# Memory keys as fp32 products in two other places, and values ahead of queries, in a one-core transformer kernel

## The reference

```python
def second_block(x, mem, ...):
    mem_n = rms_norm_2(mem, mem_norm)               # 256 tokens, the same for both layers
    for i in range(2):
        hn = rms_norm_2(x, g[0])
        t = rglru_mixer(hn, ...) if i == 0 else rwkv7_mixer(hn, ...)
        x = x + rms_norm_2(t, g[1])
        c = mem_cross_attention(rms_norm_2(x, g[2]), mem_n, w_q[i], w_kv[i], w_o[i])
        x = x + rms_norm_2(c, g[3])
        x = x + rms_norm_2(sqrelu_mlp(rms_norm_2(x, g[4]), ...), g[5])

def mem_cross_attention(h, mem_n, w_q, w_kv, w_o):  # 4 heads of 256
    q = h @ w_q
    k, v = split(mem_n @ w_kv)
    p = softmax(q k^T / 16)
    return (p v) @ w_o
```

## Time and profile before

| | us |
|---|---|
| median of 3 runs | 3943.67 (3942.07 to 3945.65) |
| the profiled execution, its own time | 3945.74 |
| its span, first to last instruction | 3943.9 |
| TensorE busy | 3699.3 (94%) |
| VectorE busy | 1699.0 (43%) |
| ScalarE busy | 1516.4 (38%) |
| GpSimd busy | 1311.4 (33%) |
| mean granted TensorE clock | 0.967 |

### The profile page before, as it was taken

The page is one execution under the profiler, slowest core; times in us unless marked ns, Lnnn a source line. Parts: engine busy times, 40 slices in busy tenths (PEclk is TensorE's granted clock), DMA queues, the critical chain, the costliest instruction groups (busy, mean ns, idle before and its releaser), DMA issues.

```text
span 3943.9 us, 47965 instructions
## 1 busy us (share of the span) xinstructions
PE 3699.3 (94%) x17594; PEld 2919.9 (74%) x17594; DVE 1699.0 (43%) x2434; ACT 1516.4 (38%) x2470; POOL 1311.4 (33%) x600
## 2 busy tenths in 40 slices
PE   8989998999898999989989799999899898999997
PEld 7777786888787777778877486888534687777886
DVE  2443447443334443764335643413456443425042
ACT  3246533332322665243324644423142233444232
POOL 4422133444343212434443243444100011443442
PEclk9989999999998999999999899999999999999999
DMA  3311122223222111222322132222123000322222
GB/s 135 99 64 49 43 70 75 96 96 102 86 94 91 49 43 49 96 75 96 101 91 101 60 103 68 101 97 96 54 75 91 28 1 6 102 92 86 96 96 80
DMA packets 100066, 308.85 MB, mean 78 GB/s; under 512 B 25920, under 2 KB 26048, under 8 KB 99520
## 3 DMA queue, kind: packets, MB, share of 16 engines
q1 hardware_dynamic: 81792, 298.90, 22.6%
q10 hardware_dynamic: 18112, 7.68, 0.8%
HBM read 301.30 MB, written 4.19 MB: 77 GB/s over the span
## 4 chain that ended last, share of the span: by engine, by line
issue 45%; PE 36%; POOL 16%; DVE 2%; ACT 1%; DVEq 0%; POOLq 0%; DMA 0%; ACTq 0%; SPq 0%
POOL ring_r L2605 16%; PE ps L437 8%; PE ps L439 8%; PE ps L438 8%; PE ps L926 2%; PE ps L1026 1%; PE ps L945 1%; PE ps L607 1%; PE ps L1094 0%; PE ps L1102 0%; PE ps L1071 0%; PE ps L1084 0%; PE ps L1062 0%; PE ps L1104 0%; PE ps L1164 0%
## 5 line engine op out<-in xcount | busy, mean ns | idle before, releaser
L2605 POOL TENSOR_TENSOR ring_r<-ring,rounded_r 128x1024 fp32r<-128x1024 f32 x520 | 1272.9, 2450 | 2128.6 <-ACT rounded_r L1207 2128.1
L437 PE MATMUL ps<-source_hi,rounded_r 128*128 128x512 f32 x2560 | 1020.3, 399 | 120.5 <-DVE X_lo L1902 31.3
L1207 ACT ACTIVATE rounded_r<-ring 128x1024 fp32r<-128x1024 f32 x520 | 550.6, 1059 | 1361.0 <-PE ps L439 1212.6
L438 PE MATMUL ps<-source_hi,ring_r 128*128 128x512 f32 x2560 | 1007.5, 394 | 0.0
L437 PEld LDWEIGHTS ps<-source_hi,rounded_r 128*128 128x128 f32 x2560 | 487.9, 191 | 238.2 <-DVE X_lo L1902 33.7
L439 PE MATMUL ps<-X_lo,rounded_r 128*128 128x512 f32 x1536 | 603.0, 393 | 0.0
L438 PEld LDWEIGHTS ps<-source_hi,ring_r 128*128 128x128 f32 x2560 | 488.1, 191 | 102.4 <-issue 2.6
L439 PEld LDWEIGHTS ps<-X_lo,rounded_r 128*128 128x128 f32 x1536 | 291.3, 190 | 61.7
L439 PE MATMUL ps<-N_lo,rounded_r 128*128 128x512 f32 x768 | 303.0, 395 | 0.0
L2162 DVE SCALAR_TENSOR_TENSOR T<-ps,PAR,T 128x511 f32<-128x511 f32 (+1 forms) x176 | 131.5, 749 | 229.5 <-ACT T L1400 214.6
L437 PE MATMUL ps<-H_hi,rounded_r 128*128 128x512 f32 x512 | 199.2, 389 | 0.0
(11 more groups left out here) (496 smaller groups left out, 5779.7 us busy)
## 6 DMA issues: line engine op xcount, KB each, us to landing
ring<-in_weights SPq DMA_DIRECT2D x560, 512.0 KB, 3.3
X<-in_x SPq DMA_DIRECT2D x2, 1024.0 KB, 7.1
out_x<-X SPq DMA_DIRECT2D x4, 512.0 KB, 2.6
SWAP<-Z ACTq DMA_DIRECT2D x4, 256.0 KB, 3.4
MEM<-in_mem ACTq DMA_DIRECT2D x1, 1024.0 KB, 4.9
diag_in<-Y ACTq DMA_DIRECT2D x8, 128.0 KB, 2.2
Z<-diag_in ACTq DMA_DIRECT2D x8, 128.0 KB
diag_out<-Z ACTq DMA_DIRECT2D x2, 512.0 KB, 4.1
```

What stands on the lines that cost most here:

```text
L437: mm(o, lh, rh, start=start, stop=False)
L438: mm(o, ll, rh, start=False, stop=False)
L1207: av(RH[:, j, :], ring[:, j, :], ACT.Copy).then_inc(w_hi, 1)
L2605: nc.gpsimd.tensor_tensor(RL[:, j, :], ring[:, j, :], RH[:, j, :].bitcast(F32), ALU.subtract).then_inc(w_lo, 1)
```

## The change

- The keys of both layers are computed as plain fp32 products from unrounded chunks: 8 tiles of 8 products of 256 columns. Layer 0's key chunks stand between the gates and lru_out (B_K0), layer 1's between the feed-forward of layer 0 and RWKV (B_K1), four tiles ahead of the mean products of `rms(7)` and four behind them.
- The memory is multiplied by its gain only. The factor 1/rms is applied to the outputs: per token along the free axis for keys (`mem_keys` on VectorE), per partition as a scale of the value copies on ScalarE. The squares are summed over the 8 tiles on VectorE first (MSUM), so the mean is one product, with two one-column products for the other layout, ahead of the last LRU input quad.
- Layer 1's keys are written to DRAM (D3) before RWKV and read back (1 MB) just before RWO.
- In the tails four of the eight value chunks come first, then the queries (now skewed), then four rounds of scores with the other four value chunks and the turning. ScalarE rounds the query chunks between the steps of `split_in` and copies the first values there.
- lru_out moves to banks 0 to 3 and is skewed; its chunks 0 and 1 are rounded behind the recurrence's last square roots, between the last splits, and no longer inside the recurrence.
- The second split of the memory (MNH, MNL) moves ahead of the RWO tiles.

The diff, cut to its core:

```diff
-MEM_TURNED = (6, 4, 4, 4)
+MEM_TURNED = (6, 6, 6, 0)
+K1_BANKS = (4, 6, 7, 5)
...
 # TensorE
+            def mem_squares():
+                pe.wait_ge(scaled, 4 + KT)
+                pe.wait_ge(mem_y, 1)
+                mm(ps[:, 5, 0:S2], cst("mean"), MSUM, start=True, stop=True)
+                for t in range(2):
+                    ins = mm(ps[:, 5, S2 + t:S2 + t + 1], MSUM[:, t * P:t * P + P], cst("mean")[:, 0:1], start=True, stop=True)
                 ins.then_inc(rms_var, 1)
+            def mem_keys(first, c, bank):
+                arrived((first + c) // RING, c % RING)
+                for k in range(KT):
+                    ins = mm(ps[:, bank, (c % 2) * S2:(c % 2) * S2 + S2], w(c % RING, k), MN[:, k, :], start=(k == 0), stop=(k == KT - 1))
+                ins.then_inc(used, 1)
...
             def tail(l):
-                gemm(B, C_MQ, AH, NL, scaled, C_LRU_IN + l * KT, SRC[f"q{l}"], 0, 3 + 6 * l)
                 pe.wait_ge(mem_lo, l + 1)
-                for i in range(C_MK // RING):
-                    for j in range(RING):
...
-                        for k in range(KT):
-                            ins = three(ps[:, j, 0:S2], wh(j, k), wl(j, k), MNH[:, k, :], MNL[:, k, :], k == 0, k == KT - 1)
...
+                for c in range(RING):
+                    values(c)
+                gemm(B + RING, C_MQ, AH, NL, scaled, C_LRU_IN + l * KT, SRC[f"q{l}"], 0, 3 + 6 * l, skewed=True,
+                     second=lambda: pe.wait_ge(mv, l * 4 + 2))
                 pe.wait_ge(scaled, 4 + C_LRU_IN + l * KT + KT)
...
+                scores2(0)
+                values(4)
+                scores2(1)
+                values(5)
+                scores2(2)
+                turned2(0)
+                values(6)
+                scores2(3)
+                turned2(1)
+                values(7)
+                turned2(2)
+                turned2(3)
                 pe.wait_ge(mv, l * 4 + 4)
...
-            gemm(B_LRU, C_LRU_IN, AH, NL, scaled, 0, SRC["lru_in"], 0, 0)
+            gemm(B_LRU, C_LRU_IN, AH, NL, scaled, 0, SRC["lru_in"], 0, 0, third=mem_squares)
...
+            pe.wait_ge(mem_hi, KT)
+            for c in range(C_MK):
+                pe.wait_ge(lru_gate, 9 + c // 2)
+                mem_keys(B_K0, c, 4 + c // 2)
+            pe.wait_ge(lru_gate, 16)
+            gemm(B_LRU_OUT, C_LRU_OUT, AH, ZL2[:, 16:24, :], t_ready, 0, SRC["lru_out"], skewed=True)
...
-            rms(7)
+            for c in range(C_MK):
+                if c == 4:
+                    for n in range(KT):
+                        pe.wait_ge(rms_sq, 7 * KT + n + 1)
+                        ins = mm(ps[:, 0, :], cst("mean"), SQX[:, n, :], start=(n == 0), stop=(n == KT - 1))
+                    ins.then_inc(rms_var, 1)
+                if c == 6:
+                    pe.wait_ge(rms_std, 7)
+                mem_keys(B_K1, c, K1_BANKS[c // 2])
...
 # ScalarE, tail(l)
                 last_slot(B // RING)
+                passed(1)
+                split_in(1 + 3 * l, gain(l, 2), 0, 1)
+                passed(2)
+                split_in(1 + 3 * l, gain(l, 2), 1, 2)
+                passed(3)
+                split_in(1 + 3 * l, gain(l, 2), 2, 5)
+                last_slot(B // RING + 1)
+                values_copied(0)
+                split_in(1 + 3 * l, gain(l, 2), 5)
...
+                exps(0)
+                act.wait_ge(used, B + B_MV1 + 1)
+                exps(1)
+                passed(B_MV1 + 1)
+                turned2(0)
+                exps(2)
+                passed(B_MV1 + 2)
+                exps(3)
+                turned2(1)
+                passed(B_MV1 + 3)
+                values_copied(1)
+                turned2(2)
+                turned2(3)
...
 # ScalarE, LRU input (c: tile) and recurrence
+                if c == 1:
+                    act.wait_ge(mem_in, 16)
+                    av(MSQ, MN, ACT.Square).then_inc(rms_sq, KT)
+                if c == 2:
+                    act.wait_ge(rms_sq, 2 * KT)
+                    for n in range(KT):
+                        av(MN[:, n, :], MN[:, n, :], ACT.Copy, scale=par2("mem_norm", n, 1)).then_inc(mem_hi, 1)
+                if c == 3:
+                    act.wait_ge(mem_hi, KT)
+                    av(MNH, MN, ACT.Copy).then_inc(mem_hi, 1)
...
-                if half:
-                    round_chunk(LRU_OUT_QUAD, 0)
-                    round_chunk(LRU_OUT_QUAD, 1)
...
+            round_chunk(LRU_OUT_QUAD, 0)
+            lru_out_high(4, 5)
+            round_chunk(LRU_OUT_QUAD, 1)
+            lru_out_high(6, 7)
             round_chunk(LRU_OUT_QUAD, 2)
             last_slot(LRU_OUT_QUAD)
-            lru_out_high(4, 5, 6, 7)
-            root(1, 0, S2)
...
+            act.wait_ge(mq, 8)
+            act.dma_start(D3, KEYS1).then_inc(keys_moved, 16)
...
             last_slot(B_RWO // RING)
+            act.dma_start(MK, D3).then_inc(keys_moved, 16)
+            av(MNH, MN, ACT.Copy).then_inc(mem_hi, 1)
             out_tiles(B_RWO, 8, gain(1, 1))
...
 # VectorE
+            def mem_keys(first, dst, bank):
+                for i in range(C_MK // 2):
+                    dve.wait_ge(used, first + 2 * i + 2)
+                    tt(dst[:, 2 * i:2 * i + 2, :], ps[:, bank[i], :].rearrange("p (k s) -> p k s", k=2),
+                       MEM_FACTOR.unsqueeze(1).to_broadcast([P, 2, S2]), ALU.mult).then_inc(mq, 1)
...
-            rms(1, MN, MN, par2("mem_norm"), S2)
+            mem_keys(B_K0, MK, range(4, 8))
...
+            mem_keys(B_K1, KEYS1, K1_BANKS)
             for m, mu in enumerate((1, 4, 5, 3, 0), 1):
```

More of the change, by code:

```diff
@@ L766, in rms_out, with gemm @@
                 mm(ps[:, 5, :], cst("mean"), SQ2[(KT - 1) % 2], start=False, stop=True).then_inc(rms_var, 1)
[L769 to L773, removed]
-                ins.then_inc(rms_var, 1)
-            def gemm(first, tiles, hi, lo, free, base, src, bank=0, event=None, before=None):
+            def mem_squares():
[4 more added lines that the diff above has]
+                    ins = mm(ps[:, 5, S2 + t:S2 + t + 1], MSUM[:, t * P:t * P + P], cst("mean")[:, 0:1], start=True, stop=True)
+                ins.then_inc(rms_var, 1)
+            def mem_keys(first, c, bank):
[3 more added lines that the diff above has]
+                ins.then_inc(used, 1)
+            def gemm(first, tiles, hi, lo, free, base, src, bank=0, event=None, before=None, skewed=False, second=None, third=None):
                 done = 0
                 if src is not None:
-                    first_quad(n_split(first), bank, hi, lo, src_lo, src, 1, (free, base), before=before)
+                    first_quad(n_split(first), bank, hi, lo, src_lo, src, 1, (free, base), before=before, skewed=skewed)
                     done = 1
+                if second is not None:
+                    second()
                 if event is not None:
@@ L1436, in late_tiles, with split_in @@
                 return () if c <= RING else range(2 * (c - RING - 1), 2 * (c - RING) + (c == KT)) if c <= KT else (c,)
-            def split_in(residual, gain):
-                for n in range(KT + 1):
+            def split_in(residual, gain, first=0, end=KT + 1):
+                for n in range(first, end):
                     if n < KT:
@@ L1493, in tail, with passed, values_copied @@
                 B = B_TAIL0 if l == 0 else B_TAIL1
-                split_in(1 + 3 * l, gain(l, 2))
-                last_slot(B // RING)
-                act.wait_ge(mem_y, KT)
-                av(MNH, MN, ACT.Copy).then_inc(mem_hi, 1)
+                def passed(c):
+                    act.wait_ge(used, B + c + 1)
+                    ahead((B + c) // RING, c % RING)
+                def values_copied(half):
+                    for t in range(2):
+                        av(MV[:, t, half * 512:half * 512 + 512], ps[:, 6 - 2 * half + t, :], ACT.Copy,
+                           scale=MEM_FACTOR_T[:, t:t + 1]).then_inc(mv, 1)
+                last_slot(B // RING)
+                passed(1)
[7 more added lines that the diff above has]
+                split_in(1 + 3 * l, gain(l, 2), 5)
                 for c in range(C_MQ):
@@ L2595, in _ @@
             output_low(RU - 1)
+            mem_low(1)
             squares(8)
@@ L2722, in tail @@
         down = _blocks(i["m_w_down_2"][l], F2T).reshape(KT, P, 2, 2, CHUNK).transpose(2, 0, 3, 1, 4).reshape(2, C_HDN, P, CHUNK)
-        return [lin(i["c_w_q_2"][l]), lin(kv[:, :D]), *rows(kv[:, D:]), lin(i["c_w_o_2"][l]),
+        first, second = rows(kv[:, D:])
+        return [first, lin(i["c_w_q_2"][l]), second, lin(i["c_w_o_2"][l]),
                 up[:HALF], down[0], up[HALF:], down[1]]
     gate = i["a_gate_w_2"][0].reshape(2, 2, 2, 2, P, 2, P).transpose(1, 0, 4, 2, 5, 3, 6).reshape(4, P, CHUNK)
-    out = [lin(i["a_w_in_2"][0]), gate, lin(i["a_w_out_2"][0]), *tail(0)]
+    keys = [lin(i["c_w_kv_2"][l][:, :D]) for l in range(2)]
+    out = [lin(i["a_w_in_2"][0]), gate, keys[0], lin(i["a_w_out_2"][0]), *tail(0), keys[1]]
```

151 lines of the change are left out of this document (63 added, 88 removed).

## The result

The changed kernel takes 3914.26 us (median of four runs, 3909.08 to 3918.07), the kernel before 3944.61 beside it: a ratio of 0.9925, 95% interval 0.9912 to 0.9938, so 30.4 us less. The forecast was 37.4 less: the sign and the places are right, the gain is 7 us too large. The profiled execution's span is 3910.9 us.

A forecast was written before the change was run, and what follows sets the result against it. TensorE, busy for 94% of the span, was taken as the bound. Two tails at -24.7, LRU +2, layer 1's keys +8 and their copies +2 give -37.4 from 3943.7: about 3906 us, range 3886 to 3926, chance 0.50.

The forecast's parts named there:

- Tails: Both layers, last N_lo to first probability-value product: 34.3 us less, N_lo 9.6 late, so 24.7 gained per tail (18.8 to 31.6).
- Blocking: Residual loop of the tails: VectorE steps with two SBUF inputs and GpSimd remainders exclude each other; last N_lo 9.6 us late altogether.
- no blocking: Rival, tails: the residual keeps its pace but for ScalarE's 2.7 us; 2 x 6.9 better, 3892; chance 0.22.
- ScalarE's order: Residual loop: four roundings and two value copies between ScalarE's splits, 5.4 us, half absorbed; last N_lo 2.7 us late.
- The rival of full blocking: Tails: all five remainders block the residual, N_lo 15.5 us late, 5 to 6 a tail worse; 3917, chance 0.22 with softmax.
- The rival by which the softmax becomes the bound: Tails: maxima, exponentials and turns become the bound, 5 to 6 us a tail worse; 3917, chance 0.22 with full blocking.
- that pair of rivals (3917): Softmax chain as the bound or a fuller blocking, in the tails: 5 to 6 us a tail worse; chance 0.22 together.
- LRU input and output: Stretch from LRU input through lru_out: ends at 2262.5 against 2260.65 before, +2 us (from -1 to +5).
- near 2223: lru_out's third tile: chunk 2, queued on ScalarE behind splits, rounded near 2220.5 and its remainder done near 2223.
- the other 174 products, 39.4: lru_out behind the third tile's wait: the remaining 174 products take 39.4 us and end at 2262.5.
- Keys of layer 1: Between feed-forward and RWKV: keys, means and four RWKV tiles take 60.8 us for 53.2, +8 with hand-overs (+5 to +11).
- Read of the second keys: Just before RWO: reading back 1 MB, two chunks by the load row, delays the RWO loads; +2 us (0 to 6.6).

The follow-up runs named there:

- experiment 1: Changed kernel, GpSimd writing zeros in place of the remainders of the first four query chunks in both tails: 3904.8 us, one run.
- experiment 5: Changed kernel with lru_out's chunk 2 rounded on ScalarE ahead of the last two splits of lru_out's input: 3905.84 us, one run.
- experiment 7: Changed kernel with layer 1's eight key tiles cut to one of their eight steps: 3899.54 us, one run.
- the first execution: The changed kernel unaltered, its first profiled execution: span 3910.9 us; from RWKV's first copy to rms_out(8) 517.39 us.
- the second: The changed kernel unaltered, executed again later: from RWKV's first copy to rms_out(8) 514.47 us.
- experiment 8: Changed kernel with the read back of layer 1's keys issued behind the sixth RWO tile, not ahead of RWO: 3906.13 us, one run.
- experiment 4: Changed kernel with layer 0's eight key tiles cut to one of their eight steps: 3907.05 us, one run.

## Why the prediction was right, and where it was not

**Tails, right.** -24.6 and -23.5 for -24.7. Both halves hold in tail 0: from the last N_lo to the first probability-value product 63.85 for 62.9, and the last N_lo 8.7 late for 9.6. Blocking was the term that decided (no blocking was the first rival): 5.4 by experiment 1 where the forecast has 6.9, and ScalarE's order 3.3 for 2.7. Tail 1 gains 1.1 less than tail 0, mostly by its wait of 1.41 for a query chunk's remainder (0.42 in tail 0). The rival of full blocking had 15.5 late. The rival by which the softmax becomes the bound is out: TensorE waits 2.50 ahead of the probability-value products, 2.12 before, and 0.78 at most between the scores. By the total alone that pair of rivals (3917) lies nearer to the measured 3914 than the forecast (3906); it is the tails' own times that tell them apart.

**LRU input and output, mis-sized: +6.6 for +2, outside its bounds.** Keys at clock 1.00, 3.48 a tile for 3.4, and the third tile's remainder "near 2223" (2223.08) came as told. But this execution's LRU began 2.26 earlier, so the remainder is 2.3 later than that by the stretch's own start. The step that failed there is the recurrence's: the forecast let remainders block the residual, but not the recurrence, whose last steps lose 4.1 us to those of lru_out's first two chunks, and ScalarE's last splits begin 150.8 after the LRU input, where they began at 151.2 before. (No run takes these two remainders away.) And "the other 174 products, 39.4" priced everything behind the wait at full clock. The keys kept TensorE busy right up to it, yet after waits of 1.32 and 2.77 the clock fell: eight products at 0.43 instead of 0.23 are 1.6 us. A wait of 0.45 for a later remainder is most of the rest. The forecast saw the queue on ScalarE that causes it all, and experiment 5 shows its price: 5.4 us. Without it the stretch is +1.1.

**Keys of layer 1, right.** +7.2 for +8; experiment 7 has 8.3 for the tiles themselves.

**Read of the second keys, met by luck.** +2 was forecast; the first execution shows +1.6, the second -1.3, and the scatter of that stretch is 4 us. The 1.6 is a fall of the clock behind a wait that was there before; the wait that the read was to lengthen went from 0.31 to 0.44 (experiment 8). What the read costs on the average stays open.

**The end.** +2.1 from layer 1's probability-value products on, not forecast. The 32 probability-value products of layer 1 took 14.00 before and 15.67 after; those of layer 0 took 15.61 and 15.67. In the eleven traced executions of the changed kernel and its variants each of the two groups takes either 13.97 (five times) or 15.4 to 15.7 (17 times), behind the same wait of 2.3 to 2.5. The clock makes the difference. Below are layer 0's group in its short form, from experiment 1's kernel, the 8 us around its start, and the 8 us around the start of the long form at 2363.37 in the changed kernel (columns as above):

```profile
2364.78 13.97 PE L888 MATMUL ps<-Z 128*128 128x512 f32 x32 [2.51 <-ACT Z L1551]
```
```profile
2364.00:2372.00 8.00, 7.22 (x17) 3.34 (x18) 2.07 (x3) 2.50 (x6) 0.00 (x0) 1.00 0.00 0
2363.00:2371.00 8.00, 7.63 (x14) 3.36 (x15) 1.38 (x2) 1.93 (x4) 0.00 (x0) 0.79 0.00 0
```

In all 17 long ones three to five products behind the wait stand about 0.85 apart at a granted clock of 0.50, where the others stand 0.43; in the five short ones the clock stays at 1.00. So 1.7 of the 2.1 is the lower clock; the change may have made the fall likelier, which so few executions can't tell.

Summed by the forecast's own terms: LRU 4.6 too low, tails 1.3 too much gained, the end 2.1; the keys and the read 1.2 and the stretch between 0.2 the other way. That is 6.6, by which these two executions miss it; the medians miss it by 7.0. Of this account 1.6 in lru_out, 1.6 at RWO and 1.7 at the end are falls of the clock behind waits of 2.3 to 2.8 us. The forecast has no term for them; that one of the three took the place of its +2 for the read is why the sum isn't further off.

## What to carry to other kernels

Work for TensorE put under another engine's chain is free as long as that chain, and not the work, sets the end: take the work out once and see whether the time moves (24.4 us cost 0.2 at the one place here, 8.3 at the other). When a load or rounding is moved beside VectorE code, look where each step's inputs lie: one input in PSUM made GpSimd's remainders harmless for it (3 us a tail). On a queue that waits, put the weights' rounding ahead of the splits that aren't ready (5.4 us here). A wait of 2.3 to 2.8 us cost another 1.6 or 1.7 here where the clock fell behind it. And where a stretch differs by 1 to 2 us between two executions, look at its granted clock before naming a cause.

## What was not expected of the hardware

- A fall of the clock to the 1.2 GHz level behind two waits of 1.32 and 2.77 us, though TensorE had been busy at clock 1.00 for over 50 us before; with waits of 0.22 and 0.29 there, in experiment 5, it stayed at 1.00.
- The same 32 fp32 products take 13.97 or 15.67 us in executions of the same code behind the same wait: behind it the clock falls to its 1.2 GHz level (17 of 22) or stays (5). Why it falls in the one execution and not in the other stays open.
- VectorE's scan is held up by a remainder as well: two scans take 2.34 in the changed kernel, and 4.39 in experiment 4, where a remainder (2214.36 to 2216.70) runs beside them; 4.49 in experiment 5, beside two.
